# Small vectors, rotation angles and bounds moved from the program's entry into the steps of the first FFN

## The reference

```python
for i in range(4):                        # first stack
    h = h + 0.5 * swiglu(rms_norm(h, norm_ffn1[i]), ...)      # D_FF = 2816
    h = h + mixer_i(rms_norm(h, norm_mix[i]))                 # stick-breaking, MoBA, MLA, stick-breaking
    h = h + 0.5 * swiglu(rms_norm(h, norm_ffn2[i]), ...)
h = rms_norm(h, final_norm)
cond = silu(c); lb = cumsum(softmax(hgrn_lower_bounds, 0), 0)
for l in range(2):                        # second stack
    m = (cond @ mod_w[l] + mod_b[l]) as nine vectors of 1024
    h = h + 0.5 * m[2] * swiglu_2(modulate(rms_norm_2(h, norm_w[l, 0]), m[0], m[1]), ...)
    h = h + m[5] * hybrid_mixer(modulate(rms_norm_2(h, norm_w[l, 1]), m[3], m[4]), positions, ...)
    h = h + 0.5 * m[8] * swiglu_2(modulate(rms_norm_2(h, norm_w[l, 2]), m[6], m[7]), ...)
```

## Time and profile before

| | |
|---|---|
| median of 3 runs | 4392.58 us |
| the profiled execution, its own time | 4395.4 us |
| its span in the profile | 4393.5 us |
| PE busy | 3927.3 us (89%), mean granted clock 0.936 |
| DVE, ACT, POOL busy | 2100.0, 1444.9, 1093.4 us |

### The profile page before, as it was taken

One profiled execution on the slowest core, in us unless ns is written; L12 is line 12 of the kernel. 1 busy time (PEld: TensorE's weight loads), 2 busy tenths in 40 slices (PEclk: granted clock), 3 DMA queues, 4 the chain that ended last, 5 costly groups with the idle time before them and its releaser, 6 DMA issues.

```text
span 4393.5 us, 45835 instructions
## 1 busy us (share of the span) xinstructions
PE 3927.3 (89%) x17295; PEld 2987.4 (68%) x17295; DVE 2100.0 (48%) x2211; ACT 1444.9 (33%) x1834; POOL 1093.4 (25%) x574
## 2 busy tenths in 40 slices
PE   4998999999998899998989975869998977776999
PEld 3865888758886688875877764854587855764477
DVE  4643766337663376643664435340445543514154
ACT  3445444233442444445433212120233421211033
POOL 3800748107481074820640001100000000200000
PEclk9999999999998999999999986789999997877999
DMA  5733767437672376743745421013454532011454
GB/s 178 243 106 120 253 201 252 125 123 252 206 253 89 99 253 206 248 129 101 249 163 180 137 83 39 1 67 134 163 191 144 172 111 69 1 67 48 153 172 134
DMA packets 493295, 649.56 MB, mean 148 GB/s; under 512 B 16123, under 2 KB 393490, under 8 KB 493138
## 3 DMA queue, kind: packets, MB, share of 16 engines
q1 hardware_dynamic: 471056, 568.52, 40.4%
q0 software_dynamic: 19584, 75.50, 4.9%
q10 hardware_dynamic: 2498, 3.39, 0.3%
HBM read 646.29 MB, written 1.05 MB: 147 GB/s over the span
## 4 chain that ended last, share of the span: by engine, by line
issue 62%; POOLq 17%; PE 10%; POOL 7%; DVE 2%; ACT 1%; DVEq 0%; ACTq 0%; DMA 0%
POOLq L540 7%; POOLq L542 5%; POOLq L544 5%; PE bank L814 3%; PE bank L1110 2%; POOL mod_zone L547 2%; POOL modrow L547 1%; PE bank L1215 1%; PE bank L1229 1%; PE bank L1231 1%; POOL modrow L529 1%; POOL mod_zone L529 1%; PE bank L793 0%; PE bank L795 0%; PE bank L794 0%
## 5 line engine op out<-in xcount | busy, mean ns | idle before, releaser
L1809 DVE TENSOR_TENSOR wproj_lo<-wproj,wproj_hi 128x2048 fp32r<-128x2048 f32 x252 | 761.1, 3057 | 128.4 <-ACT wproj_hi L1389 128.4
L786 PE MATMUL bank<-wproj,xT 128*128 128x384 f32 (+2 forms) x1728 | 646.6, 531 | 20.2 <-DMA wproj<-in_w_in 11.1
L814 PE MATMUL bank<-wproj_hi,x_hi 128*128 128x512 f32 x2112 | 539.0, 397 | 30.3 <-ACT wproj_hi L1389 16.3
L786 PEld LDWEIGHTS bank<-wproj,xT 128*128 128x128 f32 x1728 | 325.4, 193 | 312.3 <-issue 185.9
L814 PE MATMUL bank<-wproj_lo,x_hi 128*128 128x512 f32 x2112 | 534.5, 396 | 0.0
L814 PE MATMUL bank<-wproj_hi,x_lo 128*128 128x512 f32 x2112 | 525.1, 391 | 0.0
L814 PEld LDWEIGHTS bank<-wproj_hi,x_hi 128*128 128x128 f32 x2112 | 396.4, 190 | 126.9 <-issue 44.0
L504 POOL TENSOR_SCALAR rstd<-sumsq 128x1 f32<-128x1 f32 x38 | 7.2, 189 | 1908.4 <-ACT tok L1372 1908.4
L1389 ACT CAST wproj_hi<-wproj 128x2048 fp32r<-128x2048 f32 x252 | 469.7, 1911 | 6.5 <-DMA wproj<-in_ffn_w_gate_up 6.5
L814 PEld LDWEIGHTS bank<-wproj_hi,x_lo 128*128 128x128 f32 x2112 | 399.4, 189 | 84.0
L814 PEld LDWEIGHTS bank<-wproj_lo,x_hi 128*128 128x128 f32 x2112 | 387.8, 188 | 76.5
(11 more groups left out here) (386 smaller groups left out, 4803.1 us busy)
## 6 DMA issues: line engine op xcount, KB each, us to landing
wproj<-in_ffn_w_gate_up SPq DMA_DIRECT2D x336, 512.0 KB, 5.9
wdown<-in_ffn_w_down SPq DMA_DIRECT2D x132, 1024.0 KB, 5.0
wproj<-in_w_in SPq DMA_DIRECT2D x52, 1024.0 KB, 6.3
wproj<-in_ffn_w_gate SPq DMA_DIRECT2D x84, 512.0 KB, 5.0
wproj<-in_ffn_w_up SPq DMA_DIRECT2D x84, 512.0 KB, 6.2
mod_zone<-in_mod_w POOLq DMA_DIRECT2D x36, 1024.0 KB, 7.3
modrow<-in_mod_w POOLq DMA_DIRECT2D x36, 1024.0 KB, 7.6
wproj<-in_sb_w_qkv SPq DMA_DIRECT2D x48, 512.0 KB, 5.3
```

Of the source, the lines that this page charges most:

```text
L786: last = nc.tensor.matmul(proj_ps[t][:, 0:rhs.shape[2]], lhsT[:, c, t * P:(t + 1) * P], rhs[:, c, :], start=(c == 0), stop=(c == kc - 1))
L814: last = nc.tensor.matmul(proj_ps[t][:, :], rounded(x_part[of_x](c)[:, toks]), rounded(w_part[of_w][:, c, :]), start=start and c == 0, sto ...
L1809: V.tensor_tensor(rounded(wproj_lo[w.odd][:, cols]), src[:, cols], wproj_hi[w.odd][:, cols], ALU.subtract).then_inc(cols_lo, 1)
```

## The change

PE's first wait is for the identity and seven loads (three gain matrices of 32 rows each, and four vectors) instead of masks and 46 loads. It transposes one block; DVE copies it and enters the FFN at once. The 30 vectors of the second stack and the five constants are now loaded by SP, behind the down weights of step 0. Their transposes stand in PE's stream between steps 0 and 1, the rest in `besides`, called at the end of a step of the first FFN: on DVE `take_vectors` (step 0), and the former entry's operations in `constants` (lambda's sums, differences of the bounds, angles; step 1), `bounds` (step 9); on ACT `conditioning` (SiLU of c; step 0), `constants` (Sin, Exp, Exp, Ln; step 2), `bounds` (Exp; step 9). DVE waits for all results after the FFN. The gains lie in another order in `vec`, so their index changes.

```diff
 # gpsimd
             nc.gpsimd.memset(ident[:, :], 0.0)
+            nc.gpsimd.memset(vec_row[:], 0.0)
+            pool.drain()
+            nc.gpsimd.affine_select(out=ident[:, :], ...).then_inc(ident_ready, 1)
...
-            mod_load(0)
-            mod_load(1)
             for l in range(DEPTH):
                 inverse_rms_rows()
                 if l == 0:
+                    mod_load(0)
+                    mod_load(1)
                     pool.wait_ge(cond_ready, 1)
 # sync: load() of the first FFN
                     rows(f, d)
+                    if small is not None and f.j is None and f.s == 0:
+                        small()
+            def small_loads():
+                sp.wait_ge(ident_ready, 1)
+                for l in range(DEPTH_2):
...
+                    for name in ("w0", "a0", "k_k", "k_a", "ln_w", "ln_b"):
+                        row(1 + l, VEC_2[name], A[f"rwkv_{name}_2"][l])      # sp.dma_start(...).then_inc(rest_in, DMA)
...
+                sp.dma_start(freq[:, :], ...).then_inc(const_in, DMA)
...
 # tensor
+            def turn_vectors():
+                pe.wait_ge(masks_ready, 1)
+                pe.wait_ge(rest_in, REST_DMAS * DMA)
+                for i, rows in list(enumerate(VEC_ROWS))[1:]:
+                    last = nc.tensor.transpose(aux_ps[:, (i - 1) * P:(i - 1) * P + rows], vec_row[0:rows, i, :], ...)
+                last.then_inc(vec_turned, 1)
-            pe.wait_ge(masks_ready, 1)
+            pe.wait_ge(ident_ready, 1)
             pe.wait_ge(vec_in, VEC_DMAS * DMA)           # 46, now 7
-            for i, rows in enumerate(VEC_ROWS):
...
-            pe.wait_ge(vec_ready, 1)
+            nc.tensor.transpose(turn_ps[:, 0:VEC_1_ROWS], vec_row[0:VEC_1_ROWS, 0, :], ...).then_inc(vec_turned, 1)
             turn_x(0, False)
-                ffn(False, lambda: turn_x(0, False))
+                ffn(False, lambda: turn_x(0, False), besides=turn_vectors if l == 0 else None)
 # scalar
-            act.wait_ge(masks_ready, 1)
-            for l in range(DEPTH):
-                for s, name in enumerate(("norm_ffn1", "norm_mix", "norm_ffn2")):
-                    row(0, (3 * l + s) * KC, A[name][l])
+            act.wait_ge(ident_ready, 1)
+            for s, name in enumerate(("norm_ffn1", "norm_mix", "norm_ffn2")):
+                act.dma_start(vec_row[s * DEPTH * KC:(s + 1) * DEPTH * KC, 0, :],
+                              A[name].rearrange("l (r f) -> (l r) f", f=P)).then_inc(vec_in, DMA)
...
+            def conditioning():
+                act.wait_ge(vec_ready, 1)
+                nc.scalar.activation(cond[:, :], vec[:, 0, VEC_1["c"]:VEC_1["c"] + KC], ACT.Silu).then_inc(cond_ready, 1)
...
+            def bounds():
+                act.wait_ge(low_d, 2)
+                nc.scalar.activation(lows[:, 2], lows[:, 1], ACT.Exp).then_inc(low_s, 1)
-                ffn(False, l == 0, False)
+                ffn(False, l == 0, False,
+                    besides={0: conditioning, 2: constants, 9: bounds} if l == 0 else {})
 # scalar and vector, at the end of an FFN step, behind the split of the weights of step k + 2
+                    if k in besides:
+                        besides[k]()
 # vector
+            v.wait_ge(vec_turned, 1)
+            V.tensor_copy(vec[:, 0, 0:VEC_1_ROWS], turn_ps[:, 0:VEC_1_ROWS]).then_inc(vec_ready, 1)
+            v.drain()
+            def take_vectors():
+                v.wait_ge(vec_turned, 2)
+                for i, rows in list(enumerate(VEC_ROWS))[1:]:
+                    V.tensor_copy(vec[:, i, 0:rows], aux_ps[:, (i - 1) * P:(i - 1) * P + rows])
+                v.drain()
+                v.sem_inc(vec_ready, 1)
+            def constants():
+                v.wait_ge(const_in, CONST_DMAS * DMA)
+                v.wait_ge(masks_ready, 1)
...
-                return gains[:, k, :], None
+                return gains[:, k % 3 * DEPTH + k // 3, :], None
-                ffn(False, lambda: enter_mix(0, gained(3 * l + 1), False))
+                ffn(False, lambda: enter_mix(0, gained(3 * l + 1), False),
+                    besides={0: take_vectors, 1: constants, 9: bounds} if l == 0 else {})
                 enter_mix(1, gained(3 * l + 1), False)
+                if l == 0:
+                    v.wait_ge(low_s, 2)
+                    v.wait_ge(trig_ready, 1)
+                    v.wait_ge(cond_ready, 1)
```

More of the change, by code:

```diff
@@ L616, in room, with ffn @@
                     sp.wait_ge(proj_done, st.n(2, -2))
-            def ffn(gate, up, down, lead, after=None):
+            def ffn(gate, up, down, lead, after=None, small=None):
                 def columns(f, w, d, gate=gate, up=up, dst=None, behind_ffn=True):
@@ L697, in gate_up_2, with row @@
                 return A["ffn_w_gate_2"][l, k], A["ffn_w_up_2"][l, k]
+            def small_loads():
+                def row(i, at, vector):
+                    rows = vector.shape[0] // P
+                    sp.dma_start(vec_row[at:at + rows, i, :],
+                                 vector.rearrange("(r f) -> r f", f=P)).then_inc(rest_in, DMA)
+                sp.wait_ge(ident_ready, 1)
+                for l in range(DEPTH_2):
+                    whole = 14 * P
+                    row(1 + l, VEC_2["mu"], A["rwkv_mu_2"][l, 0:whole])
+                    sp.dma_start(vec_row[VEC_2["mu"] + 14:VEC_2["mu"] + 15, 1 + l, 0:P_B - whole],
+                                  A["rwkv_mu_2"][l:l + 1, whole:P_B]).then_inc(rest_in, DMA)
+                    for name in ("w0", "a0", "k_k", "k_a", "ln_w", "ln_b"):
+                        row(1 + l, VEC_2[name], A[f"rwkv_{name}_2"][l])
+                    row(1 + l, VEC_2["r_k"], A["rwkv_r_k_2"][l].rearrange("h n -> (h n)"))
+                    row(1 + l, VEC_2["subln"], A["subln_w_2"][l])
+                    row(1 + l, VEC_2["hnorm"], A["hgrn_norm_w_2"][l])
+                    for k in range(DEPTH_2):
+                        row(1 + l, VEC_2[f"bound{k}"], A["hgrn_lower_bounds_2"][k])
+                    row(1 + l, VEC_2["norm_w"], A["norm_w_2"][l].rearrange("a b -> (a b)"))
+                    row(3 + l, 0, A["mod_b_2"][l])
+                with nc.allow_non_contiguous_dma("256 positions, once"):
+                    sp.dma_start(pos_i[:, :], A["positions_2"].rearrange("b (t p) -> p (b t)", p=P)).then_inc(const_in, DMA)
+                sp.dma_start(grow[:, :], A["final_norm"].rearrange("(a d) -> a d", a=1).broadcast_to([P, D])).then_inc(const_in, DMA)
+                sp.dma_start(freq[:, :], A["rope_freq"].rearrange("(a d) -> a d", a=1).broadcast_to([P, NROPE])).then_inc(const_in, DMA)
+                sp.dma_start(qkw[:].rearrange("p a b c -> p (a b c)"), A["qk_norm_w_2"].rearrange("a b c -> (a b c)").unsqueeze(0)
+                              .broadcast_to([P, DEPTH_2 * 2 * DH_A])).then_inc(const_in, DMA)
+                sp.dma_start(lqk[:].rearrange("p a b c -> p (a b c)"), A["lambda_qk_2"].rearrange("a b c -> (a b c)").unsqueeze(0)
+                              .broadcast_to([P, DEPTH_2 * 4 * DH_A])).then_inc(const_in, DMA)
@@ L795, in split_product, with ffn @@
                 return nc.tensor.matmul(ps, rounded(a), rounded(b), start=False, stop=final, skip_group_check=True)
-            def ffn(scaled, then=None, rows={}):
+            def ffn(scaled, then=None, rows={}, besides=None):
                 def gate_up(st, w, t, mid=None, entering=False):
@@ L875, in ffn @@
                     mod_row(*rows[0])
+                if besides is not None:
+                    besides()
                 step(Step(n.ffn + 1), Step(n.load + 1), True, rows.get(1))
@@ L1722, in _ @@
             row(0, VEC_1["index"], A["token_index"])
[L1723 to L1749, removed]
@@ new lines, in constants @@
+            def constants():
+                act.wait_ge(trig_ang, 1)
+                nc.scalar.activation(trig[:], ang[:], ACT.Sin).then_inc(trig_ready, 1)
+                act.wait_ge(lam_terms, 1)
+                nc.scalar.activation(lam_e[:], lam_e[:], ACT.Exp).then_inc(lam_exp, 1)
+                act.wait_ge(low_d, 1)
+                nc.scalar.activation(lows[:, 3], lows[:, 3], ACT.Exp, scale=-1.0)
+                act.drain()
+                nc.scalar.activation(lows[:, 3], lows[:, 3], ACT.Ln, bias=1.0).then_inc(low_s, 1)
@@ L1885, in copy_even, with ffn @@
                 n.odd += (kc + 1) // 2 // 2
-            def ffn(ffn_next, then, row=None, rows={}, layer=None):
+            def ffn(ffn_next, then, row=None, rows={}, layer=None, besides={}):
                 scaled = row is not None
@@ L2439, in _ @@
[L2439 to L2458, removed]
@@ new lines, in bounds @@
+            def bounds():
+                v.wait_ge(lam_exp, 1)
+                V.tensor_tensor(lam[:, :], lam_e[:, :, 0], lam_e[:, :, 1], ALU.subtract)
+                v.wait_ge(low_s, 1)
+                V.scalar_tensor_tensor(lows[:, 1], lows[:, 0], 0.0, lows[:, 3], ALU.max, ALU.add)
+                v.drain()
```

(7 more changed lines are left out.)

100 lines of the change are left out of this document (47 added, 53 removed).

## The result

The changed kernel takes 4369.57 us (median of 12 runs, 4360.88 to 4385.86), the kernel before 4395.06 (12 runs on the same chips, 4391.52 to 4398.84): 25.5 us less, ratio 0.9945, 95% interval 0.9935 to 0.9955. The forecast was 33.6 us less. The direction was right and so was the place of the largest cost; the forecast gain was about a third larger than the measured one. The profiled execution took 4366.52 us, its span is 4364.8, 28.7 less than the span before.

A forecast was written before the change was run, and what follows sets the result against it. PE bounds the steps, and the entry is serial time in front. Terms -44.9 + 1.3 + 0.7 + 6.5 + 2.2 + 0 + 0.7 = -33.5 us gave 4361.9 profiled, 4359 as median; range 4352 to 4370.

The forecast's parts named there:

- The entry: Before the first FFN: the seven loads land at 7.4 us, DVE scales x at 8.9 instead of 53.82, 44.9 us earlier.
- The table load at the Square: In the entry on ACT, between x and the cast of the first weights: a first table load costs 1.3 us.
- Rival 5: At the entry: something it hid, such as the weights of steps 0 and 1, holds PE; gain under 9 us; chance 0.02.
- PE's transposes: Four transposes in PE's stream between steps 0 and 1 of the first FFN cost 0.7 us, their loads being there.
- rival 4: SP's small issues throttle behind the backlog, making step 2's load late: 4380 us at 1.12 each, 4406 at 1.88; chance 0.04.
- rival 1: In the entry: the seven loads queue behind SP's 6 MB, 13.7 us less gain, 4373 us; chance 0.09.
- The columns of step 2: Step 2's weights share the way with constants and modulation tiles; second half lands near 37 us; cost 0, bounds 0 and 3.
- The constants: DVE's moved operations before L1900 of step 2 stop PE without cover: 6.5 us, bounds 5.6 and 10.6.
- rival 3: The constants don't stop PE, as POOL leaves DVE alone then; stall and clock cost go, 4350 us; chance 0.05.
- The clock: PE runs at half clock behind the stall for DVE's constants: 2.2 us, bounds 0 and 4.
- ACT's constants: In step 2: four table loads and four small operations, some 6.1 us, hidden by 0.5 us; cost 0, bounds 0 and 3.
- rival 2: A change of ACT's tables costs more than its load: L1421 in step 2 comes 5.1 us later, 4364 us; chance 0.05.

The follow-up runs named there:

- e6: The changed kernel, but SP issues nothing behind x until the seven small vectors have landed: 4378.57 us (one run).
- e3: The changed kernel, but the first two modulation tiles are loaded in front of the first 1/rms again, as before: 4372.67 us, ratio 0.9946.
- e4: On top of e2, the first two modulation tiles are loaded only after step 0's products: 4355.55 us, ratio 0.9918.
- e1: The changed kernel, but GpSimd starts its first modulation part only when the angles are there: 4375.58 us, ratio 0.9950.
- e2: The changed kernel, but with the constants at the end of step 10 and the bounds behind the first FFN: 4360.70 us, ratio 0.9916.
- a0_after: The changed kernel run again with no edit: 4372.14 us, ratio 0.9943 against the kernel before.

## Why the prediction was wrong in size

The forecast gain was 33.5 us. Between the two traces it is 4.8 less, of which the constants are 4.1, the late columns of step 2 1.6 (with 0.3 less for PE's transposes) and the entry 1.4; against them stand smaller differences in the last rows of the table. The other 3.2 us are the profiled executions: that of the changed kernel was 3.0 us faster than its median, that of before 0.3 slower.

- **The entry.** Forecast 7.4 us for the landing, measured 10.07 and 9.55, 10.70, 10.80 in others: mis-sized by 2.7, inside its bounds (6.2 and 21.1). Neither bound's mechanism held alone: the queues share, and sharing costs 3 us (e6).
- **The table load at the Square** (forecast 1.3): wrong in its place. It stands in front of ACT's first cast, at 5.40 us, while ACT waits for x: 0. The two errors cancel by half: 42.2 for 43.6. Rival 5 (the weights hold PE) was wrong: ACT's cast of the first weights followed the square sums with no wait.
- **PE's transposes** (0.7): 0.4. The rivals on SP's issues (rival 4) and on the queue (rival 1) did not happen: SP issues a small load in 0.3 us.
- **The columns of step 2** (0, bounds 0 and 3): 1.9. I had put both the tiles and the constants in their way, reckoned 8 us for them where 2.9 MB at my rate (6 MB in 19 us) are 9.2, and called it no wait; the second half landed at 44 us and not at 37. e3 and e4 show that it was the tiles, moved into the way of these columns by the same edit. With the columns late, the cover that I had counted on for `take_vectors` was gone too.
- **The constants** are the step that failed: 6.5 us forecast, 10.6 measured. The place and the loop-carried chain were right, and rival 3 (no stall) was wrong in all traces. The size was not: "Bounds 5.6 and 5.6 x 1.9 = 10.6; I take **6.5**, nearer to the first as operations are small." I scaled the streaming part by the slowdown of a long subtraction. But a small operation is not slowed in proportion: it waits for GpSimd's whole instruction, of 0.7 to 4.4 us in the traces of the changed kernel. The 23 operations in a row meet four to six of these: 12.7 and 13.3 us in the two traces of the changed kernel, 13.4 in e3_mod_first, 16.8 in e6_sp_yields, all longer than the 10.6 of my upper bound. e1 and e2 show the other half, 5.7 and 5.4 us without GpSimd. The sum closes: in the first trace five operations (L2483, L2494, L2511, L2513, L2515) took 7.6 us more than in e1, and 5.7 + 7.6 = 13.3. There was some cover after all, which I had denied: the subtraction in front of the constants took 5.59 us for 8.44, so of the 13.3 us PE saw 10.4 more than its stall of before (10.93 against 0.51). That the cost at PE came out at my upper bound is luck. The hold seems to go both ways, which no run tested: while VectorE's operations followed one another without a gap, GpSimd's L543 stood 2.70 us (4.07 in a0_after) with nothing that the profile shows to wait for, and started when they paused. The Trainium skill (GPSIMD Engine Reference, Key points) says that GpSimd shares its SBUF interfaces with VectorE, in contention with instructions in a 2-port mode or with two SBUF inputs; the traces agree that there is contention, and show operations with one SBUF input among those held.
- **The clock** (2.2): 2.1, as forecast, by products of 3.78 us for 2.12.
- **ACT's constants** (0): hidden, as forecast. Its table loads follow one another with no drain of a microsecond between, so rival 2 was wrong (last three rows of the timeline of the changed kernel above). There were three loads and not four: the Sin needed none. The loads in the three rounds of the hardware loop came as forecast (the first of them is SiLU's behind these constants), and one more behind the bounds (L1465 has 11 for 7 before); none made PE wait.
- **Bounds** (0.7): 0, the product was there when PE came.
- **Behind the first FFN** nothing is given back: at the ends of the seven later FFNs of the first stack the gain lies between 28.8 and 31.8 us, and at the end of the span it is 28.7. Whether the changed kernel's runs spread more is open: its first 12 spread over 25 us, against 7 for before, but its next five over 7.2, against 14.3.

## What to carry to other kernels

Moving setup work out of a serial entry is worth its time only by the place where it lands: the same operations cost 10.6 us, with 2.1 behind them for the clock, between two steps of a loop that keeps PE busy, and nothing that the traces show in a gap of VectorE some 140 us later. Before placing small VectorE operations, look at what GpSimd runs in that stretch, and count one of its whole instructions for each meeting, not a percentage. And a shift of one engine's work moves its DMAs too: here the tiles slid from in front of the columns of step 2 into their midst.

## What the runs showed of the hardware

- A VectorE TENSOR_SCALAR on 128x4 elements, 0.16 us alone (e1), took 3.86 us beside a GpSimd TENSOR_TENSOR of 3.62 us (the changed kernel).
- PE's clock after a stall: eight 128x512 products took 3.5 to 3.8 us behind each stall of 3.2 us and more in front of a step of the first FFN. Behind shorter ones it was open: 2.10 (e4) and 2.78 us (e2) behind 1.87 us of idleness, 2.12 behind 2.17 (e1), 2.88 behind 2.23 (e2), 2.47 behind 1.03 (e3). The length of the stall alone doesn't tell it. In e3 the eight products lost 0.35 us behind a stall of 1.03, in a0_after 1.5 behind one of 3.22.
- Four issues of 512 KB on SP took 2.1 us (e4) when GpSimd issued its 2 MB of tiles after them, and 8.8 us (the changed kernel) with these tiles under way.
